# A two-layer diffusion block on one core: the neighbourhood bias and column mask move from VectorE to TensorE

## What is computed

```python
key_rows = clip(r - kh // 2, 0, rows - kh)[:, None] + arange(kh)        # kh = rows = 8: all rows
key_cols = clip(arange(4) * 16 - 8, 0, 64 - 32)[:, None] + arange(32)   # 32 key columns for 16 query columns
col_in = (key_cols >= win_start) & (key_cols < win_start + 16)
bias = rpb[:, dr, dc]                                # by row distance and column distance
s_loc = q @ k_nb * scale + bias
s_loc = where(valid, s_loc, -1e30)                   # valid: col_in
s_ctx = q @ k_ctx * scale
p = softmax(concatenate([s_loc, s_ctx]))
```

## Time and profile before

| what | value |
|---|---|
| median of 3 executions | 1784.51 us |
| the profiled execution's own time | 1784.84 us |
| its span, first to last instruction | 1783.0 us |
| TensorE busy | 1665.5 us (93%) |
| VectorE busy | 959.8 us (54%) |
| ScalarE busy | 663.4 us (37%) |
| GpSimd busy | 784.2 us (44%) |
| mean granted TensorE clock | 0.978 of 2.4 GHz |
| B steps of layer 0 | about 375.7 to 408 us of the span |
| B steps of layer 1 | about 1316.6 to 1347.3 us of the span |

### The profile page before, as it was taken

The page is one execution under the profiler, slowest core; times in us unless marked ns, Lnnn a source line. Parts: engine busy times, 40 slices in busy tenths (PEclk is TensorE's granted clock), DMA queues, the critical chain, the costliest instruction groups (busy, mean ns, idle before and its releaser), DMA issues.

```text
span 1783.0 us, 27785 instructions
## 1 busy us (share of the span) xinstructions
PE 1665.5 (93%) x10959; PEld 1229.3 (69%) x10959; DVE 959.8 (54%) x1715; ACT 663.4 (37%) x1218; POOL 784.2 (44%) x576
## 2 busy tenths in 40 slices
PE   7999988977989999999899998997887999999998
PEld 3688877866856678666776687886776645645646
DVE  4434498894458851686418844457995612112112
ACT  3222367774243320243013113226875354053130
POOL 2234345652523553345414342551334557468363
PEclk9999999999989999999999998998999899999999
DMA  9355542313124523345225422554003224333332
GB/s 317 48 129 141 131 128 79 90 49 83 36 82 132 149 65 95 95 130 154 59 84 172 148 71 48 144 132 109 16 1 89 78 71 119 94 96 105 83 83 83
DMA packets 317279, 179.11 MB, mean 100 GB/s; under 512 B 88526, under 2 KB 310494, under 8 KB 317150
## 3 DMA queue, kind: packets, MB, share of 16 engines
q1 hardware_dynamic: 284542, 143.63, 30.7%
q10 hardware_dynamic: 32608, 33.71, 6.1%
HBM read 158.97 MB, written 2.83 MB: 91 GB/s over the span
## 4 chain that ended last, share of the span: by engine, by line
PE 60%; DVE 5%; POOL 2%; issue 2%; ACT 2%; SPq 1%; DMA 0%; DVEq 0%; ACTq 0%; POOLq 0%
PE acc L890 55%; PE small L1161 1%; DVE act L1612 1%; DVE stat L1774 1%; DVE prob_t L1788 1%; POOL split_w L656 1%; DVE scaled_ffn L1626 1%; PE side L1071 0%; POOL pair_w L762 0%; PE mod_ps L987 0%; ACT prob_t L1413 0%; DVE o_sum L1800 0%; PE side L880 0%; SPq L546 0%; ACT prob L1391 0%
## 5 line engine op out<-in xcount | busy, mean ns | idle before, releaser
L890 PE MATMUL acc<-act,pair_w 128*128 128x512 f16 x3168 | 581.1, 345 | 6.7 <-ACT act L1277 4.2
L890 PEld LDWEIGHTS acc<-act,pair_w 128*128 128x128 f16 x3168 | 307.6, 98 | 270.1 <-DVE act L1612 9.4
L890 PE MATMUL acc<-act,split_w 128*128 128x512 f32 (+1 forms) x1920 | 378.1, 355 | 9.1 <-DVE act L1874 2.9
L890 PEld LDWEIGHTS acc<-act,split_w 128*128 128x128 f32 x1920 | 307.6, 190 | 61.8 <-DVE act L1874 4.8
L890 PE MATMUL acc<-hidden,split_w 128*128 128x512 f32 (+1 forms) x1584 | 310.9, 358 | 10.6 <-issue 6.3
L890 PEld LDWEIGHTS acc<-hidden,split_w 128*128 128x128 f32 x1584 | 261.3, 189 | 57.7 <-issue 7.1
L653 POOL TENSOR_SCALAR split_w<-raw_w 128x1024 fp32r<-128x1024 f32 (+1 forms) x120 | 126.0, 1050 | 396.3 <-PE acc L890 301.8
L656 POOL TENSOR_TENSOR split_w<-raw_w,split_w 128x1024 fp32r<-128x1024 f32 (+1 forms) x120 | 278.3, 2319 | 10.0
L759 POOL TENSOR_SCALAR pair_raw<-pair_raw,weight_scale 128x1024 f32<-128x1024 f32 x88 | 105.8, 1202 | 356.8 <-ACT pair_w L1462 356.8
L1937 DVE SCALAR_TENSOR_TENSOR mod_acc<-mod_chunk,silu_c,mod_acc 128x256 f32<-128x256 f32 x280 | 228.1, 857 | 4.0
L1637 DVE SCALAR_TENSOR_TENSOR x_t<-acc,mod,x_t 128x512 f32<-128x512 f32 x96 | 60.3, 658 | 254.1 <-PE acc L890 253.6
(11 more groups left out here) (188 smaller groups left out, 1831.8 us busy)
## 6 DMA issues: line engine op xcount, KB each, us to landing
mod_chunk<-in_w_mod ACTq DMA_DIRECT2D x28, 1024.0 KB, 5.4
pair_raw<-in_w_gate SPq DMA_DIRECT2D x44, 512.0 KB, 4.1
pair_raw<-in_w_up SPq DMA_DIRECT2D x44, 512.0 KB, 5.5
raw_w<-in_w_in SPq DMA_DIRECT2D x64, 256.0 KB, 3.7
raw_w<-in_w_down SPq DMA_DIRECT2D x32, 512.0 KB, 3.8
raw_w<-in_w_mod SPq DMA_DIRECT2D x24, 512.0 KB, 4.1
mod_start<-in_w_mod SPq DMA_DIRECT2D x8, 1024.0 KB, 12.1
ks<-q_split SPq DMA_DIRECT2D x64, 96.0 KB, 2.2
```

Of the source, the lines that this page charges most:

```text
L890: mm = pe.matmul(acc[slot][:, a:b], weights[:, part == 2, k, :], moving[:, part == 1, k, a:b], start=(k == 0 and part == 0), stop=(k == n ...
```

## The change

The bias tables, the addition on VectorE and the semaphore `biased` go. For each head GpSimd now splits the scaled `wide` into `wide_hi` (fp32r) and `wide_lo` (the remainder, written over `wide`), and once in each layer makes an fp32r identity and the column masks in bf16. TensorE adds three matmuls of 256 columns, each with an identity as the stationary operand, to the local piece of each B step: the mask (bf16), `wide_hi` and `wide_lo` (fp32r). The last two read their moving operand in the order "p c r": from one element to the next it steps 48 fp32 values (192 bytes).

```diff
-        bias = [place(f"bias{i}", [P, 3, 256], F32, a0 + 18624 + i * 3072) for i in range(4)]
+        wide_hi = place("wide_hi", [P, 4, ROWS, 48], F32R, a0 + 18624)
+        mask16 = place("mask16", [P, 3, 256], BF16, a0 + 24768)
+        ident_r = place("ident_r", [P, P], F32R, a0 + 26304)
         stat = place("stat", [P, 4, 96], F32, a0 + 30912)
         wide = place("wide", [P, 4, ROWS, 48], F32, a0 + 32448)
+        wide_lo = place("wide_lo", [P, 4, ROWS, 48], F32R, a0 + 32448)
...
-                    pool.wait_ge(bias_x8, l * 4 + h + 1)
-                    pool.tensor_tensor(bias[h][:, i - 1, :].rearrange("p (c r) -> p r c", r=ROWS),
-                                       wide[:, h, :, BIAS_AT[i - 1]:BIAS_AT[i - 1] + 32],
-                                       columns[:, i - 1:i, :].broadcast_to((P, ROWS, 32)), ALU.add
-                                       ).then_inc(bias_ready, 1)
+                    if i == 1:
+                        pool.wait_ge(bias_x8, l * 4 + h + 1)
+                        pool.tensor_scalar(wide_hi[:, h, :, :], wide[:, h, :, :], 1.0, 0.0, ALU.mult, ALU.add).then_inc(bias_hi, 1)
+                    elif i == 2:
+                        pool.wait_ge(bias_hi, l * 4 + h + 1)
+                        pool.tensor_tensor(wide_lo[:, h, :, :], wide[:, h, :, :], wide_hi[:, h, :, :].bitcast(F32), ALU.subtract
+                                           ).then_inc(bias_ready, 1)
+                    elif h == 0:
+                        pool.tensor_scalar(ident_r[:, :], ident[:, :], 1.0, 0.0, ALU.mult, ALU.add).then_inc(bias_ready, 1)
+                        for var in range(3):
+                            pool.tensor_scalar(mask16[:, var, :].rearrange("p (c r) -> p r c", r=ROWS),
+                                               columns[:, var:var + 1, :].broadcast_to((P, ROWS, 32)), 1.0, 0.0, ALU.mult, ALU.add
+                                               ).then_inc(bias_ready, 1)
...
-                        mm = pe.matmul(out_, q, ks[:, s["k"], 1, k0:k0 + size], start=False, stop=not masks)
+                        near = s["bias"] and first is not None
+                        mm = pe.matmul(out_, q, ks[:, s["k"], 1, k0:k0 + size], start=False, stop=not masks and not near)
+                        if near:
+                            var, h = VARIANT[s["qb"]], s["head"]
+                            pe.wait_ge(bias_ready, 8 * l + 5 + h)
+                            cols = slice(BIAS_AT[var], BIAS_AT[var] + 32)
+                            pe.matmul(out_, ident16[:, :], mask16[:, var, :], start=False, stop=False)
+                            pe.matmul(out_, ident_r[:, :], wide_hi[:, h, :, cols].rearrange("p r c -> p c r"), start=False, stop=False)
+                            mm = pe.matmul(out_, ident_r[:, :], wide_lo[:, h, :, cols].rearrange("p r c -> p c r"), start=False, stop=True)
...
-                    if s["bias"]:
-                        var = VARIANT[s["qb"]]
-                        ve.wait_ge(bias_ready, 12 * l + 3 * s["head"] + 3)
-                        part = acc[g % 2][:, CTX:CTX + 256]
-                        ve.tensor_tensor(part, part, bias[s["head"]][:, var, :], ALU.add).then_inc(biased, 1)
-                        ve.wait_ge(biased, upto(g + 1, is_biased))
```

More of the change, by code:

```diff
@@ L158, in upto @@
     return sum(what(s) for s in STEPS[:g])
-def is_biased(s):
-    return s["bias"]
 def mod_steps():
@@ L365, in trunk @@
         v_ps, v_ready, v_hi = sem("v_ps"), sem("v_ready"), sem("v_hi")
-        scores, biased, sink_set, top, neg_top, exps = (
-            sem("scores"), sem("biased"), sem("sink_set"), sem("top"), sem("neg_top"), sem("exps"))
+        scores, sink_set, top, neg_top, exps = (
+            sem("scores"), sem("sink_set"), sem("top"), sem("neg_top"), sem("exps"))
         r_denom, prob_ps, prob_hi, prob_lo, o_ps, o_ready = (
@@ L370, in trunk @@
         o_summed = sem("o_summed")
-        bias_x8, bias_ready = sem("bias_x8"), sem("bias_ready")
+        bias_x8, bias_hi, bias_ready = sem("bias_x8"), sem("bias_hi"), sem("bias_ready")
         ot_ps, ot_hi, ot_lo = sem("ot_ps"), sem("ot_hi"), sem("ot_lo")
```

## The result

The changed kernel takes **1791.09 us** (median of 10 runs, 1784.3 to 1794.89) against 1783.89 us of the kernel before on the same chip: ratio **1.0035, 95% interval [1.0023, 1.0048]**, or 4 to 9 us slower (the ratio gives 6.2 us, the two medians lie 7.2 apart). That lies inside the range of the prediction, but not where it was centred: 1786.0, with "no difference" as the likeliest, was too low by 5 us, and the 0.36 of the chance that lay on "slower by over 0.3%" is the case that came, though not by rival 2, which carried most of it. The profiled execution took 1790.0 us.

A forecast was written before the change was run, and what follows sets the result against it. VectorE was taken to bound the two attention stretches, TensorE close behind. Removed additions against TensorE's new matmuls summed to 25x - 13.5, +1.5 us at x = 0.60, giving 1786.0 us; range 1779.5 to 1796.

The forecast's parts named there:

- rival 2: TensorE's strided read costs as much extra per element as VectorE's: m = 0.44, x = 0.99, +11 us, 1795; chance 0.33.
- m: Time of one fp32r matmul of 256 columns with strided read on TensorE: 0.24 us, forecast 0.2 to 0.32.
- x: Time the three new TensorE matmuls add to each neighbourhood step: 0.60 us, with 0.38 below and 1.47 above.
- 5.95 + 3x: Layer 1, TensorE's group of four steps in us: 4 x (1.22 + x) plus the sum-of-outputs wait, 1.07 - x.
- rival 1: The strided read costs TensorE nothing: m = 0.133, x = 0.38, -4.0 us, 1780.5; chance 0.25.
- GpSimd: edits at nothing: GpSimd's splitting, identity and mask copies (at most 0.70 us each) add nothing; one layer 1 exponential up to 1 us late.
- if the time moves elsewhere than in these two stretches: Sign of a wrong prediction: time moving outside the two stretches of 32 attention steps, about 32 us each.
- Rival 3: First neighbourhood step of layer 0: a late table stalls TensorE; each head 2 us late gives about 1790; chance 0.03.
- The sum for layer 0: Layer 0's stretch: 32.3 us before, 26.0 + 13x after, so 33.8 at x = 0.60, a loss of 1.5 us.
- The loop score, maximum, exponential, score: Ring across engines in neighbourhood steps: 3.4 us for two steps at x = 0.60, against 3.9 taken anyway.
- rival 4: Additions cost more than 0.45 us, or identical identities load for less: x near 0.3, -6 us, 1778.5; chance 0.03.
- 25x - 13.5: Both layers' stretches together: total change in us, break-even at x = 0.54, +1.5 us at x = 0.60.

The follow-up runs named there:

- a1: Changed kernel with both fp32r matmuls reading 256 neighbouring values, bias values misplaced; ratio 1.0001 to the kernel before.
- a3: Changed kernel without the matmul for the low part of the bias; ratio 1.0010 to the kernel before.
- a2: Changed kernel with GpSimd writing the three column masks in plain order, masks misplaced; ratio 1.0018 to the kernel before.
- b3: Kernel before with the changed kernel's three mask copies added on GpSimd and not used; ratio 1.0014 to the kernel before.
- b1: Changed kernel with masks and fp32r identity made once by VectorE, none by GpSimd, later tiles moved 704 bytes; ratio 1.0042 to the kernel before.
- a4: Kernel before with VectorE's bias addition left out and nothing in its place; ratio 0.9958 to the kernel before.
- b4: Changed kernel with an addition of 256 zeros put back on VectorE; ratio 1.0036 to the kernel before.
- c2: As c1, with bias rows column-major so fp32r matmuls read 256 neighbouring values, no other tile moved; ratio 0.9992 to the kernel before.
- c1: Changed kernel with GpSimd copying 96 mask values, each read eight times by TensorE, no other tile moved; ratio 1.0031 to the kernel before.

## Why the prediction was right in its mechanism and too low in its sum

**What held.**

- *The read with a step.* m = 0.24 us was predicted; the low part measured 0.24, both parts together 0.43, so 0.21 each, with 0.12 for the plain read (0.133 predicted). VectorE's ratio of 1.83 was a good stand-in for TensorE's 1.8 to 2.0; that it carries over from one engine to another was a guess that came out. VectorE's extra per element, my rival 2, would have given 0.44.
- *x.* 0.54 instead of 0.60, the difference all in the two fp32r matmuls if the mask takes its 0.11.
- *The bound moves to TensorE, with a rest of the wait.* 0.46 us of the wait for the sum of outputs remains, 0.5 predicted and 1.07 - 0.54 = 0.53 by the formula.
- *5.95 + 3x.* At x = 0.54, 0.35 and 0.31 (after, a1, a3) it gives 7.57, 7.00 and 6.88; the groups of layer 1 took 7.69, 7.07 and 7.02. The slope is right, the constant 0.1 too low.
- *Against rival 1* (the step costs nothing): 0.24, not 0.13. a1, where it does cost nothing, also shows that its gain was put too high: at x = 0.35 the neighbourhood steps of both layers gain 2.8 us, where the sum gives 25 x 0.35 - 13.5 = -4.8.

**What failed.**

1. **"GpSimd: edits at nothing."** This is the step that failed most: +2.8 us with no term in the sum (2.25 of delay, 0.6 at the lower clock). I bounded a mask copy by the table addition, 0.70 us each, because both write 256 values with a step. The copies took 1.21 us each, and my "one exponential up to 1 us late, once" became 2.3 us late. The difference I passed over is what is written: 2-byte values 16 bytes apart here, 4-byte values 32 bytes apart there. That this is the reason is argued: a2 shows only that the order of writing makes the 2-byte copies slow. a2 and b3 show the size of the loss from both sides. In layer 0 GpSimd has no negated maxima to deliver, and the same copies cost nothing that shows: the record of the last one ends at 374.35, where I had put 372.7 at the latest, TensorE's first mask matmul starts at 375.29 without a wait, and b1, which has no copies, loses as much in this stretch (+2.25) as the changed kernel (+2.22). By the prediction's own sign ("if the time moves elsewhere than in these two stretches") it was wrong here. Rival 3, a late table, did not come, with 0.9 us to spare.
2. **The sum for layer 0.** At the x found it gives 33.0 - 32.3 = +0.7 us; the groups took 34.67 - 32.90 = +1.8, as the stretch does once the first addition is counted. Groups with a modulation took 9.06 us, which is 7.69 + 1.37: the modulation came on top in full, and the wait for the sum of outputs was still there behind it (0.46 in the rows above). So "less the wait 1.07 - x that one of them fills" was wrong by 0.5. The first group took 8.46, 0.6 less than the next, where I had put 1.1 for short context steps: another 0.5. The rest, 0.65, is the constant (0.12 x 4) and the modulation (3 x 0.09), less 0.1 at the fold. That is 1.7 us too little for the layer afterwards, of which 0.6 cancels, since the 32.3 us before were too few as well.
3. **Layer 1.** Predicted -0.7 at x = 0.54, measured +0.1 in the groups and, with the first addition, in the stretch: the same constant, and a first group of 8.41 us where I had 7.6. It took 8.17 before.
4. **The loop score, maximum, exponential, score "has two slots"** and does not bind: true at x = 0.54, false as a general bound. The loop that a4 shows runs through the high and the low part and has a floor of 6.8 us a group in layer 1. It makes the sum's gain of 13.5 us at x = 0 too large by 6, and bounds rival 4: some 7.5 us is all that was to be had.

Terms 1 to 3 add up to what the stretches show: 2.8 + (1.8 - 0.7) + (0.1 + 0.7) = 4.7 us above the 25x - 13.5 = 0 that the sum gives at x = 0.54. The prediction stood at +1.5, because x had been put too high by 0.06, so part of the nearness is luck: two errors of 1.5 and 4.7 us against each other. It was 3.2 us too low by the stretches and 5 by the medians; the rest, 1.5 to 2 us, is inside the interval and has no cause here.

## What to carry to other kernels

Before moving a term from one engine to another, work out what the removal is worth alone: here a4 says 7.5 us, and b4 says some 2 us of it are left once TensorE has the work with its scattered reads. Even the plain read of c2 leaves a gain of only 2.9 us by the stretches, which the measured time does not tell from none. Where an operand must be transposed by its access pattern, put the pattern on the engine that has slack and on the fewest instructions (16 writes of GpSimd, not 64 reads of TensorE), and price a small copy by the row of the same type and step, not by the same count of elements. An engine that stands in a chain for a 0.27 us instruction is no free engine: what is put between two of these must be shorter than the gap, and in c1 the gap is 1.7 us (1286.57 to 1288.31), where the changed kernel put 3.9. And a new tile can cost more than the work it holds: a comparison within 0.5% should keep the addresses of all other tiles, or include a kernel that only moves them. Last, begin a stretch that two kernels are compared in before the first instruction that the edit touches: mine began one addition late, and hid 0.9 us.

## What was not expected of the hardware

- Tiles moved by 704 bytes: 6.6 us, in the matmuls that read 32-bit operands (358 to 361 ns and 355 to 357 in all, 357 to 359 and 352 to 354 at the full granted clock), none in the 16-bit ones; moved by 1024 bytes: nothing that the runs tell from none.
- GpSimd writing 256 bf16 values 16 bytes apart: 1.21 us each for three in a row, against 0.38 side by side. Writing 384 fp32r values 32 bytes apart: 0.89, against 0.51. Per value the step costs 3.2 ns more in the first case and 1.0 in the second.
- TensorE reading fp32r values 192 bytes apart: 0.24 us for 256 of them from start to start, against 0.12 side by side (a1).
- One wait of TensorE of 2.2 us (2.6 in b3), with the granted clock at 1.2 GHz for 3.4 us behind it in two of the five executions that have it (after and b3; not a1, a3 and b4).
- TensorE reading a bf16 operand with each value eight times in a row: 272 ns, as for 256 plain values.
